# Ten of a tile's nineteen left-over V groups moved from beside the attention to beside the recurrence, and a few dots moved the other way

## The chip, the cores and the metric

The kernel runs on one core of one Trainium2 chip. The metric is the device time of one execution in microseconds (us); lower is better. The five engines of the core work side by side, each through its own list of instructions in order: TensorE (PE, with its weight loads as PEld), VectorE (DVE), ScalarE (ACT), GpSimd (POOL) and SyncE (SP). An engine waits for another one only where its list holds a wait on a semaphore. Sixteen DMA engines move the data between the chip's memory and the on-chip memories.

## What is computed

One inference step of an encoder with one layer: 16 meta tokens, 512 prompt tokens and 64 sample tokens go through a norm and one input projection; eight attention heads and, beside them, four heads of a gated recurrence; an output projection and a residual; then a retrieval layer. Cut to what matters here, the retrieval of one tile of tokens is:

```python
q = (xb @ w_query).reshape(T, 8, 2, 128)
s = einsum('thcd,hcnd->thcn', q, sub_keys)          # scores against 2 x 128 keys
sa, ia = top_k(s[:, :, 0], 16); sb, ib = top_k(s[:, :, 1], 16)
...                                                 # best 16 of the 256 sums per head -> eidx (128 per token), gate
act = gelu(einsum('thkd,td->thk', expert_u[eidx], xb))   # one dot product per token and slot: row of U
return einsum('thk,thkd->td', gate * act, expert_v[eidx]) # weighted sum of rows of V
```

Each token picks 128 of 16384 experts, and each expert is a row of 1024 floats in U and one in V. So every tile of 128 tokens fetches 128 x 128 rows of U and as many of V, at addresses that are known only after the top-k.

## The kernel before

The tokens are cut into five tiles: tile 0 holds the sample and the meta tokens, tiles 1 to 4 hold 128 prompt tokens each. All engines run a loop over the tiles `t = 0..4`. A pass of it has these stages, which I name here as the tables in the code do: `start` and `head0` to `head7` (the attention, eight heads), `subtract`, `levels`, `multiply`, `masks` and `gram0` to `gram3` (the recurrence, done in chunks with one set of Gram matmuls per head), `out` (output projection), `rows` (norm, query projection, scores) and `top` (the top-k, on DVE).

The retrieval of a tile is carried out inside the passes that follow. One gather (POOL, an indirect DMA, line 589 for U and 595 for V) brings one row for each of 128 tokens: 128 x 4096 bytes = 0.524 MB. A U gather is used up by one **dot** on DVE (line 1384, a multiply with a sum over 1024 columns). Four V gathers are used up by one **V group** (the code says quad): ACT makes four 128x32 diagonals out of the weights (line 817, a ring of 8), and PE runs matmuls with them over the rows (line 1041), summing into PD. A tile has 128 U gathers and 32 V groups (tile 0 half of each).

In pass `t` stand: the dots of tile `t-1`, spread over the stages by `DOT_PLACES`; at `top`, the first 13 V groups of tile `t-1` (16 in pass 1, all of tile 0's); and in passes 3 and 4 the other 19 V groups of tile `t-2`, spread by `LEFT_PLACES`. Pass 1 has half the dots, with each number halved and rounded down, and `rows` gets what is left. What is left of tiles 3 and 4 comes after the last pass.

All gathers are issued by POOL in one order, which is worked out from the two tables, and land in a ring of slots; a gather waits until the dot or V group that used its slot before has been done:

```python
quads = len(of_values) // QUAD
for i in range(max(1, quads)):
    for k in of_keys[len(of_keys) * i // max(1, quads):len(of_keys) * (i + 1) // max(1, quads)]:
        u_place[k] = len(order)
        order.append((t, k, None))
    for n in of_values[i * QUAD:(i + 1) * QUAD]:
        v_place[n] = len(order)
        order.append((t, None, n))
...
    slot = i % FIRST_RING if i < SLOTS // 2 else (i - SLOTS // 2 + FIRST_RING) % RING
```

So inside a place the dots are dealt out over its V groups, the ring has `RING = 17` slots (for the 64 dots of pass 1 only `FIRST_RING = 5`), and a tile's first gather also waits for `chosen`, the end of that tile's top-k.

What stands around the moved work, by engine: PE does in a head `scores` (line 1099), `turn_probs` (1110), the head's V groups, `values` (1118). Then come the transposes for the recurrence (1153 to 1157), the V groups of `levels`, a transpose (1165) that waits for `lev_mul`, the V groups of `masks`, and per recurrent head the Gram matmuls (1181, 1182) and, one head later, its outputs (1189, 1191); V groups of `gram1` and `gram2` stand between the outputs of one head and the Gram matmuls of the next. DVE masks and reduces a head's Gram (1519, 1521) and then does the dots of that place; the Gram matmuls of the next head wait for the reduce. ACT does the exponential of the recurrence (903) behind the diagonals of `levels`, and copies the finished sum PD out (914) behind those of `gram2`.

Of the kernel before, what the change touches and what calls it, by code (L numbers as in the profile page):

```python
# [37 lines left out]
HEADS = 8  # L38
# [3 lines left out]
HG = 4  # L42
# [36 lines left out]

DOT_PLACES = [("start", 7)] + [(f"head{h}", 7) for h in range(HEADS)] + [
    ("subtract", 3), ("levels", 5), ("multiply", 3), ("masks", 4)] + [(f"gram{h}", 3) for h in range(HG)] + [
    ("out", 12), ("rows", 26)]
LEFT_PLACES = [("start", 2)] + [(f"head{h}", 2) for h in range(HEADS)] + [
    ("levels", 1)]
NEXT_PLACES = [("top", 13)]

FIRST_NEXT = 16
# [24 lines left out]
def build(nc, x_prompt, x_sample, cache_kt, cache_v, cache_logf, state_hgrn, meta_tokens, w_in,  # L114
# [4 lines left out]
    with ExitStack() as ctx:  # L119
# [205 lines left out]
        def columns_of(t):  # L325

            first = (S_GROUPS + T_GROUPS * (t - 1)) * GROUP
            return range(first, first + SLOTS) if t else range(SLOTS // 2)
# [17 lines left out]
        def values_before(t):  # L346

            return SLOTS // 2 + SLOTS * (t - 1) if t else 0
# [6 lines left out]
        for t in range(1, TILES):  # L355
            cols, taken = columns_of(t - 1), 0
            for place, n in DOT_PLACES:
                n = n * len(cols) // SLOTS if place != DOT_PLACES[-1][0] else len(cols) - taken
                dots_at[t, place] = cols[taken:taken + n]
# [4 lines left out]
            if t > 2:  # L364
                first, left, quads_before = values_before(t - 2) + n_next, SLOTS - n_next, 0
                of_tile = (values_before(t - 1) - first) // QUAD
                for place, quads in LEFT_PLACES:
                    taken = of_tile * quads_before * QUAD // left
# [16 lines left out]
        for t in range(1, TILES + 1):  # L385
            for place in [place for place, _ in DOT_PLACES + NEXT_PLACES] + ["end", "last", "rest"]:
                of_keys, of_values = dots_at.get((t, place), ()), values_at.get((t, place), ())
# [1330 lines left out]
```

## Time and profile before

| | us |
|---|---|
| time, median of 3 runs | 2190.84 (2189.47 to 2190.89) |
| the profiled execution: its own time | 2188.74 |
| its span, first to last instruction | 2186.6 |
| DVE busy | 1261.9 |
| PE busy | 1222.7 |
| POOL busy | 1166.5 |
| ACT busy | 372.6 |
| data moved by DMA | 722.04 MB, 330 GB/s over the span |

No engine is busy for more than 58% of the span. The granted TensorE clock was 0.738 of full speed on the mean. Of the 722 MB, 624.01 went through the queue that the gathers use. What is between the span and the execution's time (2.1 us) is not part of the trace.

### The profile page before, as it was taken

How to read it: one execution, taken by the hardware profiler on the slowest of the kernel's cores; microseconds unless marked ns; L12 is line 12 of the kernel's file. 1: busy time of each engine (PE TensorE's matmuls, PEld its weight loads, DVE VectorE, ACT ScalarE, POOL GpSimd, SP SyncE). 2: the span in 40 equal slices, each digit the busy share in tenths (PEclk: the TensorE clock that was granted, in tenths of full speed). 3: DMA queues.
4: the chain of work that ended last, by engine and by line, in shares of the span. 5: the costliest groups of instructions: out<-in, count | busy, mean ns of one | idle time of the engine just before them, and what ended most of it. 6: DMA issues, size and time to landing. Idle time of an engine off the chain costs nothing.

```text
span 2186.6 us, 15704 instructions
## 1 busy us (share of the span) xinstructions
PE 1222.7 (56%) x4932; PEld 548.7 (25%) x4932; DVE 1261.9 (58%) x2795; ACT 372.6 (17%) x1034; POOL 1166.5 (53%) x1197
## 2 busy tenths in 40 slices
PE   5898777555864436744553675466467322223553
PEld 2544343234321333311123331123323000000110
DVE  3344331866595997765439786544977656565001
ACT  1221211121121111311111131111113100001211
POOL 3012110232477754577774457777445767777773
PEclk9798889776998567866656786666578656555787
DMA  9211183556899989999998999999899999999997
GB/s 331 99 59 59 58 297 119 186 201 221 331 410 409 409 331 397 378 377 409 409 409 328 397 390 376 409 409 409 305 397 352 374 409 409 409 410 409 411 409 294
DMA packets 204306, 722.04 MB, mean 330 GB/s; under 512 B 23248, under 2 KB 25536, under 8 KB 203072
## 3 DMA queue, kind: packets, MB, share of 16 engines
q0 software_dynamic: 171168, 624.01, 73.5%
q1 hardware_dynamic: 33056, 97.03, 12.2%
q8 instruction: 40, 0.66, 0.1%
q14 instruction: 42, 0.34, 0.0%
HBM read 704.71 MB, written 15.70 MB: 329 GB/s over the span
## 4 chain that ended last, share of the span: by engine, by line
DMA 26%; PE 24%; DVE 16%; POOL 13%; issue 5%; ACT 4%; DVEq 0%; POOLq 0%; ACTq 0%
DMA arena<-peer_expert_v,idx_v 16%; POOL arena L595 8%; DMA arena<-peer_expert_u,idx_all 7%; DVE arena L1384 7%; PE PD L1041 5%; POOL arena L589 4%; PE PB L1251 4%; PE PD L963 3%; PE PB L1230 2%; PE PA L1181 2%; PE PA L1230 2%; DMA lev<-w_out 2%; DMA lev<-peer_w_query 2%; DVE w L1521 2%; PE PA L1041 1%
## 5 line engine op out<-in xcount | busy, mean ns | idle before, releaser
L589 POOL DMA_INDIRECT arena<-peer_expert_u,idx_all x576 | 542.5, 942 | 507.7 <-DVE arena L1384 259.6
L1384 DVE SCALAR_TENSOR_TENSOR arena<-arena,PC 128x1024 f32<-128x1024 f32 x576 | 677.1, 1217 | 142.8 <-DMA arena<-peer_expert_u,idx_all 135.6
L595 POOL DMA_INDIRECT arena<-peer_expert_v,idx_v x576 | 567.3, 985 | 228.7 <-issue 143.1
L1041 PE MATMUL PD<-arena,diag_v 128*32 128x512 f32 x1792 | 365.6, 897 | 497.6 <-DMA arena<-peer_expert_v,idx_v 436.5
L1041 PEld LDWEIGHTS PD<-arena,diag_v 128*32 128x32 f32 x1792 | 80.0, 141 | 749.8 <-issue 749.8
L817 ACT ACTIVATE diag_v<-consts,gate_all 128x32 f32<-128x32 f32 x576 | 136.7, 309 | 535.0 <-PE PD L1041 410.7
L963 PE MATMUL PD<-arena 128*128 128x512 f32 x384 | 174.6, 610 | 0.0
L1449 DVE TENSOR_TENSOR PA<-PA,consts 128x128 f32<-128x128 f32 (+4 forms) x56 | 14.0, 250 | 219.9 <-PE PA L1099 219.6
L1041 PE MATMUL PA<-arena,diag_v 128*32 128x512 f32 x512 | 85.5, 800 | 80.3 <-DMA arena<-peer_expert_v,idx_v 80.3
L963 PEld LDWEIGHTS PD<-arena 128*128 128x128 f32 x384 | 73.4, 196 | 85.9 <-issue 85.3
L1230 PE MATMUL PB<-lev,rows_t 128*128 128x512 f32 x160 | 83.0, 672 | 11.0 <-ACT rows_t L922 5.6
L1251 PE MATMUL PB<-arena,rows_t 128*128 128x512 f32 (+1 forms) x160 | 81.8, 676 | 5.6 <-ACT rows_t L926 5.6
L1118 PE MATMUL PB<-v_pr,w 128*128 128x64 f32 (+1 forms) x224 | 52.1, 378 | 48.4 <-ACT w L876 48.4
L857 ACT ACTIVATE w<-PA,small 64x576 f32<-64x576 f32 (+5 forms) x48 | 25.2, 526 | 294.0 <-DVE small L1452 287.6
L1230 PE MATMUL PA<-lev,rows_t 128*128 128x512 f32 (+1 forms) x160 | 72.5, 600 | 4.9 <-DMA lev<-peer_w_query 4.9
L1644 DVE TENSOR_TENSOR lev<-lev,PD 128x1024 f32<-128x1024 f32 x1 | 1.2, 1222 | 126.3 <-PE PA L1041 126.3
L1181 PE MATMUL PA<-lev 128*128 128x128 f32 x248 | 52.3, 394 | 34.4 <-DVE w L1521 34.4
L1118 PEld LDWEIGHTS PB<-v_pr,w 128*128 128x128 f32 (+1 forms) x224 | 43.6, 268 | 82.6 <-ACT w L876 53.1
L1181 PEld LDWEIGHTS PA<-lev 128*128 128x128 f32 x248 | 48.6, 297 | 38.2 <-DVE w L1521 23.1
L1165 PE MATMUL PB<-consts,lev 128*128 128x128 f32 x20 | 5.4, 426 | 94.0 <-DVE lev L1512 94.0
L1041 PEld LDWEIGHTS PA<-arena,diag_v 128*32 128x32 f32 x512 | 18.8, 131 | 147.8 <-issue 147.8
L648 POOL DMA_DIRECT2D arena<-w_in x4 | 3.6, 899 | 93.0 <-PE PD L963 93.0
(271 smaller groups left out, 1527.4 us busy)
## 6 DMA issues: line engine op xcount, KB each, us to landing
lev<-w_out SPq DMA_DIRECT2D x40, 512.0 KB, 8.1
lev<-peer_w_query SPq DMA_DIRECT2D x40, 512.0 KB, 8.1
arena<-w_in SPq DMA_DIRECT2D x8, 2048.0 KB, 14.3
arena<-peer_expert_u,idx_all POOLq DMA_INDIRECT x576, 11.2
arena<-peer_expert_v,idx_v POOLq DMA_INDIRECT x576, 11.4
arena<-w_in POOLq DMA_DIRECT2D x4, 2048.0 KB, 8.8
act<-staged SPq DMA_DIRECT2D x4, 1796.0 KB
staged<-arena POOLq DMA_DIRECT2D x5, 1024.0 KB, 5.5
```

The source lines that it names most:

```text
L589: pool.indirect_dma_start(slot, None, peer_expert_u[0], bass.IndirectOffsetOnAxis(ap=idx_all[:, k:k + 1], axis=0)).then_inc(arrived, 16)
L595: pool.indirect_dma_start(slot, None, peer_expert_v[0], bass.IndirectOffsetOnAxis(ap=idx_v[:, k:k + 1], axis=0)).then_inc(arrived, 16)
L817: return eng.activation(diag_v[:, at * STRIP:(at + 1) * STRIP], consts[:, C_FOLD:C_FOLD + STRIP], ACT.Copy, scale=gate_all[:, k:k + 1])
L857: eng.activation(w1[0:m, D * (a % 2):D * (a % 2) + n], score_psum(a, n)[0:m, :], ACT.Exp, bias=negmax[0:m, h:h + 1], accum_out=psums[0:m, ...
L963: last = pe.matmul(out, x[:, c * P:(c + 1) * P], weights[:, c, :], start=(c == 0), stop=(c == DC - 1))
L1041: ins = pe.matmul(psum[c * STRIP:(c + 1) * STRIP, half * 512:(half + 1) * 512], diag_v[:, at * STRIP:(at + 1) * STRIP], ring[slot_of[v_pla ...
L1118: last = pe.matmul(attended(t)[0:m, h * HD:(h + 1) * HD], w2[0:k, at:at + m], value_rows(t, q0, i, k, h // (HEADS // KV_HEADS)), start=(i ...
L1181: pe.matmul(psum[:, l * P:(l + 1) * P], both, both, start=True, stop=True)
L1230: last = pe.matmul(out[:, half * 512:(half + 1) * 512], rows_t[:, c % DC * P:c % DC * P + n], w_out_sb[:, slot, half * 512:(half + 1) * 51 ...
L1251: last = pe.matmul(PB[0:nq, half * 512:half * 512 + 512], rows_t[:, c * P:c * P + nq], w_query_sb[:, c, half * 512:half * 512 + 512], star ...
L1384: eng.scalar_tensor_tensor(out=slot, in0=slot, scalar=1.0, in1=h2_dots[:, :], op0=ALU.mult, op1=ALU.mult, accum_out=out).then_inc(free, 1)
L1521: eng.tensor_reduce(w1[:, D + HW + h * P:D + HW + (h + 1) * P], masked[:, c0:D].rearrange("p (l q) -> p q l", q=P), AX_X, ALU.add).then_in ...
```

## The change

Two tables of numbers change, nothing else:

```diff
-DOT_PLACES = [("start", 7)] + [(f"head{h}", 7) for h in range(HEADS)] + [
-    ("subtract", 3), ("levels", 5), ("multiply", 3), ("masks", 4)] + [(f"gram{h}", 3) for h in range(HG)] + [
-    ("out", 12), ("rows", 26)]
-LEFT_PLACES = [("start", 2)] + [(f"head{h}", 2) for h in range(HEADS)] + [
-    ("levels", 1)]
+DOT_PLACES = [("start", 8)] + [(f"head{h}", 8) for h in range(HEADS)] + [
+    ("subtract", 2), ("levels", 4), ("multiply", 2), ("masks", 3)] + [(f"gram{h}", 2) for h in range(HG)] + [
+    ("out", 12), ("rows", 25)]
+LEFT_PLACES = [("start", 1)] + [(f"head{h}", 1) for h in range(HEADS)] + [
+    ("levels", 3), ("masks", 3), ("gram1", 2), ("gram2", 2)]
```

Counted out per pass (dots + V groups, and the gathers that these are):

| pass | attention | recurrence | out | rows |
|---|---|---|---|---|
| 1 before | 27 dots | 10 dots | 6 | 21 |
| 1 after | 36 dots | 9 dots | 6 | 13 |
| 2 before | 63 dots | 27 dots | 12 | 26 |
| 2 after | 72 dots | 19 dots | 12 | 25 |
| 3 and 4 before | 63 dots + 18 groups = 135 gathers | 27 dots + 1 group = 31 gathers | 12 | 26 |
| 3 and 4 after | 72 dots + 9 groups = 108 gathers | 19 dots + 10 groups = 59 gathers | 12 | 25 |

POOL in pass 3, from `head7` on (U gathers by line 589, V gathers by 595; the last row of before also holds the later stages). Before:

```order
L589 DMA arena<-peer_expert_u,idx_all 128x1024 x3
L595 DMA arena<-peer_expert_v,idx_v 128x1024 x4
L589 DMA arena<-peer_expert_u,idx_all 128x1024 x4
L595 DMA arena<-peer_expert_v,idx_v 128x1024 x4
L589 DMA arena<-peer_expert_u,idx_all 128x1024 x8
L595 DMA arena<-peer_expert_v,idx_v 128x1024 x4
L589 DMA arena<-peer_expert_u,idx_all 128x1024 x57
```

With the change, from `head7` to the first group of `masks`:

```order
L589 DMA arena<-peer_expert_u,idx_all 128x1024 x8
L595 DMA arena<-peer_expert_v,idx_v 128x1024 x4
L589 DMA arena<-peer_expert_u,idx_all 128x1024 x3
L595 DMA arena<-peer_expert_v,idx_v 128x1024 x4
L589 DMA arena<-peer_expert_u,idx_all 128x1024
L595 DMA arena<-peer_expert_v,idx_v 128x1024 x4
L589 DMA arena<-peer_expert_u,idx_all 128x1024 x2
L595 DMA arena<-peer_expert_v,idx_v 128x1024 x4
L589 DMA arena<-peer_expert_u,idx_all 128x1024 x3
L595 DMA arena<-peer_expert_v,idx_v 128x1024 x4
```

A head's gathers went from 7 U and 8 V to 8 U and 4 V, and V gathers now stand between those of the recurrence's dots.

PE in pass 3 from the V groups of `levels` to the third head's Gram matmuls. Before:

```order
L1041 MATMUL PD<-arena,diag_v 32x512 x8
L1165 MATMUL PB<-consts,lev 128x128 x4
L1181 MATMUL PA<-lev 128x128 x7
L1182 MATMUL PA<-w 128x128
L1181 MATMUL PA<-lev 128x128 x7
L1182 MATMUL PA<-w 128x128
L1189 MATMUL PB<-act,w 128x128
L1191 MATMUL PB<-state,lev 128x128
L1181 MATMUL PA<-lev 128x128 x7
```

With the change:

```order
L1041 MATMUL PD<-arena,diag_v 32x512 x24
L1165 MATMUL PB<-consts,lev 128x128 x4
L1041 MATMUL PD<-arena,diag_v 32x512 x24
L1181 MATMUL PA<-lev 128x128 x7
L1182 MATMUL PA<-w 128x128
L1181 MATMUL PA<-lev 128x128 x7
L1182 MATMUL PA<-w 128x128
L1189 MATMUL PB<-act,w 128x128
L1191 MATMUL PB<-state,lev 128x128
L1041 MATMUL PD<-arena,diag_v 32x512 x16
L1181 MATMUL PA<-lev 128x128 x7
```

Three V groups (8 instructions each here, 16 in the trace) now stand ahead of the first Gram matmuls, and two ahead of those of the third head; two more stand ahead of the fourth's.

DVE in pass 1, around the dots of `rows`, as a piece of the difference:

```order
 L1561 SCALAR_TENSOR_TENSOR rows<-w,small 128x1024
-L1384 SCALAR_TENSOR_TENSOR arena,dots_all<-arena,PC 128x1024 x21
+L1384 SCALAR_TENSOR_TENSOR arena,dots_all<-arena,PC 128x1024 x13
 L1401 TENSOR_TENSOR dots_all<-dots_all,gate_all 128x64
 L1577 MAX lev<-PB 128x8 x8
```

Eight of tile 0's dots left this place for the attention of pass 1.

## Rows read from the trace of the kernel before

**Rows 1.** The page's slices: GB/s in 40 equal slices of the span.

```profile
GB/s 331 99 59 59 58 297 119 186 201 221 331 410 409 409 331 397 378 377 409 409 409 328 397 390 376 409 409 409 305 397 352 374 409 409 409 410 409 411 409 294
```

**Rows 2.** Stretches: length, busy PE, PEld, DVE, ACT, POOL; granted clock, DMA share, GB/s.

```profile
685.30:766.30 81.00, 29.37 (x104) 22.08 (x104) 80.40 (x154) 9.06 (x33) 61.16 (x66) 0.54 1.03 409
969.00:1146.40 177.40, 87.40 (x406) 31.59 (x406) 84.05 (x154) 26.03 (x105) 133.36 (x143) 0.63 1.03 409
1146.40:1159.50 13.10, 6.03 (x29) 2.83 (x28) 9.13 (x23) 2.34 (x6) 4.25 (x5) 0.63 1.02 404
1159.50:1174.75 15.25, 0.00 (x0) 0.00 (x0) 15.21 (x35) 4.04 (x1) 10.78 (x11) 0.50 0.92 330
1174.75:1203.00 28.25, 16.50 (x80) 15.80 (x80) 27.48 (x34) 1.51 (x2) 13.14 (x15) 0.74 0.82 296
1203.00:1213.80 10.80, 2.93 (x12) 2.63 (x12) 8.72 (x21) 3.57 (x5) 2.82 (x3) 0.66 0.95 356
1350.40:1530.20 179.80, 97.55 (x445) 40.00 (x446) 85.27 (x162) 28.51 (x105) 134.11 (x143) 0.69 1.03 409
1530.20:1598.20 68.00, 25.60 (x121) 20.81 (x120) 60.48 (x110) 11.47 (x14) 29.62 (x31) 0.55 0.87 314
```

**Rows 3.** Costliest groups: the wait of the V groups on PE.

```profile
L1041 PE MATMUL PD<-arena,diag_v 128*32 128x512 f32 x1792 | 365.6, 897 | 497.6 <-DMA arena<-peer_expert_v,idx_v 436.5 <-ACT diag_v L817 61.1
```

**Rows 4.** Order of time, PE in pass 3: start, us, what, [idle before].

```profile
1138.25 3.50 PE L1041 MATMUL PD<-arena,diag_v 128*32 128x512 f32 x16 [5.03 <-DMA arena<-peer_expert_v,idx_v]
...
1174.89 1.09 PE L1165 MATMUL PB<-consts,lev 128*128 128x128 f32 x4 [17.64 <-DVE lev L1512]
...
1182.59 3.33 PE L1181 MATMUL PA<-lev 128*128 128x128 f32 x14 [3.31 <-DVE w L1521]
1185.71 0.45 PE L1182 MATMUL PA<-w 128*128 128x128 f32 x2
...
1203.04 0.80 PE L1189 MATMUL PB<-act,w 128*128 128x128 f32 x2 [2.78 <-DVE w L1521]
```

**Rows 5.** Order of time, DVE in pass 3.

```profile
1153.06 1.21 DVE L1384 SCALAR_TENSOR_TENSOR arena<-arena,PC 128x1024 f32<-128x1024 f32 x1
1154.20 1.21 DVE L1384 SCALAR_TENSOR_TENSOR arena<-arena,PC 128x1024 f32<-128x1024 f32 x1
...
1159.43 1.21 DVE L1384 SCALAR_TENSOR_TENSOR arena<-arena,PC 128x1024 f32<-128x1024 f32 x1
...
1179.31 1.22 DVE L1519 TENSOR_TENSOR w<-PA,level_masks 128x1024 f32<-128x1024 f32 x1
```

**Rows 6.** Order of time, POOL in pass 3.

```profile
1154.55 0.94 POOL L589 DMA_INDIRECT arena<-peer_expert_u,idx_all  x1 [6.48 <-DVE arena L1384]
...
1165.89 1.15 POOL L589 DMA_INDIRECT arena<-peer_expert_u,idx_all  x1 [0.30 <-issue]
...
1289.52 0.94 POOL L595 DMA_INDIRECT arena<-peer_expert_v,idx_v  x1 [14.98 <-PE PD L1041]
...
1320.50 2.50 POOL L595 DMA_INDIRECT arena<-peer_expert_v,idx_v  x1 [0.31 <-issue]
```

**Rows 7.** DMA issues: KB each, median us from issue to landing.

```profile
arena<-peer_expert_u,idx_all POOLq DMA_INDIRECT x576, 11.2
...
w<-x_prompt SPq DMA_DIRECT2D x4, 512.0 KB, 4.1
```

**Rows 8.** The chain that ended last: one V group.

```profile
1303.61 1.98 PE PD L1041 x16
```

**Rows 9.** Order of time in pass 1: DVE at `head6`, POOL and PE at `top`.

```profile
461.77 0.30 DVE L1449 TENSOR_TENSOR PA<-PA,consts 128x128 f32<-128x128 f32 x1 [3.86 <-PE PA L1099]
...
606.68 0.94 POOL L595 DMA_INDIRECT arena<-peer_expert_v,idx_v  x1 [0.48 <-PE PD L1041]
...
670.26 0.94 POOL L595 DMA_INDIRECT arena<-peer_expert_v,idx_v  x1 [0.30 <-issue]
...
680.22 3.63 PE L1041 MATMUL PD<-arena,diag_v 128*32 128x512 f32 x16 [1.49 <-DMA arena<-peer_expert_v,idx_v]
```

## The prediction, made before the changed kernel was run

> **What bounds the kernel now.** I began with the page's slices: from a quarter of the span on, the DMA engines move 409 to 411 GB/s in most slices and never more, so that is their ceiling here; single slices fall to 305 to 397 [rows 1]. A gather is 0.524 MB, so at 409 GB/s one takes 1.28 us. The costliest groups say who feels it: V groups on PE waited 437 us for their rows, the longest wait of a group [rows 3]. Then I cut passes 2, 3 and 4 into stages [rows 2]. The attention of passes 3 and 4 runs at 409 GB/s from end to end (177.4 and 179.8 us), though DVE and PE are busy for half of it: it is as long as its 135 gathers. The recurrence behind it is another case: 404, 330, 296 and 356 GB/s in pass 3 and 314 on the mean in pass 4, and DVE is busy for nearly all of it (15.21 of 15.25 us, 27.48 of 28.25). It has 31 gathers and room for more. So the change takes gathers from where DMA sets the end to where it doesn't. The last views are lists in order of time, for the recurrence of pass 3.
>
> **Passes 3 and 4: attention.** It loses 27 gathers of 1.28 us: 34.6 us. Does it stay bound by DMA? A head has 8 dots, of which one starts every 1.14 us [rows 5], thus 9.1 us, beside 12 gathers, 15.4 us: yes. On before's clock the attention of pass 3 now ends at 1146.4 - 34.6 = 1111.8, and its last V rows, which PE waited for until 1138.25 [rows 4], land at 1103.6.
>
> **Passes 3 and 4: recurrence.** It has 57 gathers up to the last V row of `gram2`, 73 us at the ceiling. What can starve the DMA is the ring: a gather needs the slot of the one 17 places ahead. POOL stood for 6.48 us until the first dot of `subtract` gave its slot back [rows 6], and yet the stretch moved 404 GB/s [rows 2]: what was in flight covered it. The tightest place now is the first dot of `levels` (place 111 of the pass): it runs at 1159.43 [rows 5] less 34.6, less one dot of `subtract` (1.14), and frees its slot at 1124.9. Gather 128, which waits for it, would land at 1103.6 + 20 x 1.28 = 1129.2 if nothing starved. How long a gather takes from issue to landing when few others are in flight, no row shows: between 4.1 us (a load of as many bytes that is issued into a quiet queue) and the 11.2 us median of gathers [rows 7]. That makes a loss of 0 to 6.9 us; I take 1.5, near the quiet end, since the queue is nearly empty by then. So gather 128 lands at 1130.7 and the last V row of `masks`, 15 later, at 1149.9.
>
> From there PE's order counts, since the groups stand ahead of the Gram matmuls. A group takes 3.5 to 3.6 us [rows 4, 9] at the low clock; a head's Gram matmuls 3.57 (1182.59 to 1186.16) and its outputs 0.8 [rows 4]; DVE's mask and reduce 3.28 (1179.31 [rows 5] to PE's start at 1182.59 [rows 4]). In order: third group of `masks` 1153.5; Gram of head 0 1157.1; reduce 1160.3; Gram of head 1 1163.9; outputs 1164.7; two groups of `gram1`, whose rows have landed (1149.9 + 12 x 1.28 = 1165.3 for the second) 1171.9; Gram of head 2 1175.5 (its reduce was done at 1167.2); outputs 1176.3; groups of `gram2` 1179.9 and 1183.5 (last row landed at 1178.1); Gram of head 3 1187.1; reduce 1190.4. Before, that reduce let PE go on at 1203.04 [rows 4]: -12.6 us. One dot fewer in `gram3` gives between nothing and 1.14, as PE's last matmuls run beside it: -0.5. Against it, the five loads of w_out that are issued here meet gathers that before had landed: +1.0 (bounds in the rival of the debt, below), and gathers beside DVE's products are issued more slowly: +0.5 (below). Pass 3: **-11.6**. Pass 4 has the same gathers, and from its attention to the end of its recurrence it took 68.0 us where pass 3 took 67.4 [rows 2]: **-11.6**.
>
> ACT's 12 diagonals of `levels` stand ahead of its exponential and wait for PE's first group there, whose rows land at 1103.6 + 7 x 1.28 = 1112.6; the exponential's input comes at about 1123.7, and that time hides them. Were the group later than that, DVE's products would be late by as much. SP's list is the same, and no queue is passed. The 26th dot of `rows` isn't on a path: PE's projections end that stage.
>
> **Pass 2 pays.** It has no left-over groups, so it only gets 9 dots more beside the attention, which DVE fills (80.40 of 81.00 us [rows 2]): 9 x 1.14 = +10.3. Its recurrence loses 8 dots: one each in `subtract`, `levels` and `multiply`, which are DVE's chain (-3.4); one in `masks` and one per Gram, beside which PE's Gram matmuls run (3.57 against 3 dots of 1.14: 0), but 0.5 for the last. Sum **+6.4**; bounds +1.2 (all eight on the path) and +10.3.
>
> **Pass 1 is nearly even.** DVE waits 3.86 us per head for PE's item projections [rows 9], which covers the fourth dot, but not in `start`, `head6` and `head7`: +3.4, and +0.6 because only five slots serve them (0 to 2). In `rows` eight dots fewer are of no use to PE, but POOL comes to the V gathers some 10 us earlier (8 x 1.28). The 18th of them, however, waited for PE's first group even before (0.48 us at 606.68 [rows 9]); so the 64th is issued at 670.26 as now, and only its landing gets shorter: 10.0 us now (PE had waited for it until 680.22), 4.1 at best [rows 7]. Gain 0 to 5.9; I take 3. Sum **+1**.
>
> Sum: +1 + 6.4 - 11.6 - 11.6 = -15.8, so 2188.74 - 15.8 = 2172.9 against the profiled execution. That execution is 2.1 us below the median of the runs, so I forecast **2175 us**.
>
> The 0.5 for slower issue: beside DVE's large products of the top-k a gather's issue took 2.50 us instead of 0.94, beside the short products of the recurrence 1.15 [rows 6]. Some five issues per pass meet such products; by the row they lose 0.2 us each at most, 1.0, and I took half. The Trainium skill (SBUF — State Buffer, "Who interferes with whom") has a rule that speaks against gathers in this place: a DVE instruction with two SBUF inputs and a GpSimd instruction that reads SBUF exclude each other. By it I estimate that each of the five waits out a whole product of 0.4 us: 2 us per pass, and 2178 in all.
>
> **The rivals.**
> *A faster PE* (0.2). A V group took 1.98 us where PE had worked just before [rows 8]. The granted clock was 0.74 beside the Gram matmuls and 0.50 (1.2 GHz) in the stretch without matmuls before them [rows 2]; groups in that stretch may lift it. Then the groups no longer hold PE, and the last rows do: 1178.1 + 2.0 + 3.6 + 3.3 = 1187.0 for the last reduce, 3.4 us more per pass, 2168. The Trainium skill (TensorE: Matmul & The Clock Gate, Part 1) has the clock released by activity, which would go this way.
> *The ring starves the DMA* (0.1, the slow side). If the stretch keeps the rate that it had, 330 GB/s for 56.6 us of pass 3 [rows 2], its 57 gathers (29.9 MB) take 90.6 us instead of 74.6: +16 in each pass, 2207. It decides from 7.9 us per pass on, that is below 362 GB/s. For it speaks POOL's stop of 6.48 us; against it, that DVE was busy all through: the rate was low since few rows were asked for.
> *The debt comes due* (0.08). Before, all 17 slots hold landed rows when the recurrence ends; then about 9, and 8 x 1.28 = 10.3 us of DMA work is left to stages that run at 400 and more. If `out` and the projections wait for all of it, both passes keep 2.3 us: 2194, no change. Against it: POOL stood idle for 14.98 us until 1289.52 with a full ring, before the next V groups began [rows 6]; that is where the debt can be paid.
> Other (0.05): the change does nothing because another wait takes over in the attention, e.g. DVE behind PE's group.
>
> **Numbers.** Forecast as summed 0.57, 2166 to 2185. This measurement tells about 0.2%, 4.4 us, from no change. Faster 0.8 (forecast, faster PE, a little of the rest), same 0.1, slower 0.1. Range 2163 to 2188: from the faster PE with all of the gain in pass 1 and a little more in pass 2, to 6.5 us lost per pass in the ring; the slow rivals lie above.
>
> **What would show it.** Right: attention of passes 3 and 4 about 143 and 145 us at 409 GB/s; from its end to the last reduce about 78 us instead of 57, at 385 GB/s or more; the attention of pass 2 91 us; PE's groups in `masks` waiting for DMA and those in `gram1` not. Wrong: POOL standing for over 8 us in the recurrence, released by the dots of `levels` or of a Gram; `out` longer by over 4 us; or DVE dots, not V rows, ending a head.

## The result and the profile after

The changed kernel takes **2177.36 us** (median of 5 runs, 2174.77 to 2179.58), the kernel before 2190.89 in the same job: ratio 0.9925, 95% interval 0.9909 to 0.9941. It is faster by 13.5 us on the medians and by 10.7 us between the profiled executions (2178.01 and 2188.74; spans 2175.9 and 2186.6). The 3 us between these two are chance: the attention of pass 0, which the tables don't touch, took 107.96 us in the profile of before, 111.86 in that of after, and 110.65 in the control with the tables of before (below).

Cut at PE's last transposes of the queries (line 1060), the profiles give per pass:

| | before | after | difference | predicted |
|---|---|---|---|---|
| ahead of pass 1 | 389.72 | 392.99 | +3.3 | 0 |
| pass 1 | 295.56 | 296.74 | +1.2 | +1 |
| pass 2 | 283.74 | 292.09 | +8.4 | +6.4 |
| pass 3 | 381.37 | 369.18 | -12.2 | -11.6 |
| pass 4 and what follows, to DVE's last instruction | 833.08 | 821.76 | -11.3 | -11.6 |

The tables don't touch what stands ahead of pass 1, so its 3.3 us are no effect of the change; passes 1 to 4 together gained 13.9 us.

The windows that answer to [rows 2], with the same columns: attention of pass 2; attention, `subtract` with `levels` up to the products, `multiply`, Grams, mix and `out` of pass 3; attention, its end to the last reduce, and `out` of pass 4.

```profile
689.71:781.03 91.32, 29.61 (x105) 22.13 (x104) 90.69 (x172) 9.96 (x34) 69.08 (x74) 0.53 1.03 409
981.80:1122.37 140.57, 59.20 (x262) 25.33 (x262) 92.45 (x172) 18.41 (x69) 106.44 (x113) 0.62 1.03 409
1122.37:1134.42 12.05, 7.81 (x45) 3.72 (x44) 8.01 (x22) 4.15 (x14) 4.23 (x5) 0.77 1.02 398
1134.42:1147.41 12.99, 2.74 (x16) 0.50 (x16) 12.96 (x31) 4.05 (x1) 9.13 (x9) 0.64 0.86 311
1147.41:1200.39 52.98, 32.98 (x192) 15.37 (x192) 23.22 (x27) 8.09 (x30) 39.88 (x44) 0.77 1.02 408
1200.39:1210.12 9.73, 1.60 (x12) 1.42 (x12) 7.63 (x20) 3.57 (x5) 5.86 (x6) 0.81 1.03 410
1210.12:1238.65 28.53, 19.55 (x40) 8.69 (x40) 14.93 (x26) 2.31 (x2) 11.32 (x12) 0.77 1.03 410
1350.98:1495.24 144.26, 64.46 (x305) 31.57 (x305) 94.84 (x180) 20.91 (x69) 109.11 (x116) 0.66 1.03 409
1495.24:1572.26 77.02, 44.91 (x250) 20.11 (x248) 44.17 (x76) 16.29 (x45) 53.84 (x57) 0.73 1.01 398
1582.73:1609.86 27.13, 20.98 (x40) 9.01 (x40) 14.92 (x26) 2.31 (x2) 11.32 (x12) 0.77 1.03 410
```

The attention of pass 3 lost 36.8 us (177.4 to 140.6) and still stands at the ceiling. The stretch of the Grams, which ran at 296 GB/s, runs at 408 and takes 52.98 us instead of 28.25. The mix (the last step of the recurrence, ahead of `out`) went from 356 to 410 GB/s. And `out`, where nothing was moved, is new on the list: 28.53 us. Its window of before, not shown so far, has 21.99:

```profile
1213.80:1235.79 21.99, 18.25 (x40) 7.96 (x40) 14.91 (x26) 2.31 (x2) 11.27 (x12) 0.86 1.00 403
```

Out of these two windows: 410 x 28.53 us = 11.70 MB were moved in it after, 403 x 21.99 = 8.86 MB before. The 2.84 MB more take 6.9 us at 410 GB/s.

What waits there, on PE, in order of time as in [rows 4]. First before, then after; line 1230 is the output projection, in blocks of w_out of which each is four matmuls:

```profile
1216.96 10.33 PE L1230 MATMUL PB<-lev,rows_t 128*128 128x512 f32 x20 [1.11 <-ACT rows_t L922]
1227.46 1.98 PE L1230 MATMUL PB<-lev,rows_t 128*128 128x512 f32 x4 [0.17 <-DMA lev<-w_out]
1230.00 1.98 PE L1230 MATMUL PB<-lev,rows_t 128*128 128x512 f32 x4 [0.56 <-DMA lev<-w_out]
```

```profile
1213.27 10.48 PE L1230 MATMUL PB<-lev,rows_t 128*128 128x512 f32 x20 [1.11 <-ACT rows_t L922]
1230.30 7.10 PE L1230 MATMUL PB<-lev,rows_t 128*128 128x512 f32 x12 [6.55 <-DMA lev<-w_out]
```

The first five blocks are there in time. The sixth is late by 6.55 us; the two behind it come just as PE gets to them. SP's own list, in order of time, says what stands ahead of that block (after):

```profile
1200.43 0.33 SPq L517 DMA_DIRECT2D w<-x_prompt  x1
1201.20 2.23 SPq L525 DMA_DIRECT2D lev<-w_out  x5
1210.16 0.33 SPq L534 DMA_DIRECT2D w<-norm_gain  x1
1210.53 0.43 SPq L537 DMA_DIRECT2D act<-sub_keys_t  x1
1216.91 3.76 SPq L525 DMA_DIRECT2D lev<-w_out  x3
```

How long some of these took to land (after; KB each, us from issue): the fifth block (issued at 1203.0), the gain, the keys, the sixth block:

```profile
lev<-w_out SPq DMA_DIRECT2D x1, 512.0 KB, 18.4
w<-norm_gain SPq DMA_DIRECT2D x1, 512.0 KB, 13.7
act<-sub_keys_t SPq DMA_DIRECT2D x1, 1024.0 KB, 17.2
lev<-w_out SPq DMA_DIRECT2D x1, 512.0 KB, 13.3
```

So they landed one behind the other, at 1221.4, 1223.9, 1227.7 and 1230.2: between the fifth and the sixth block 6.3 us went to the gain and the keys. PE was through with the fifth block at 1223.75; without these 6.3 us the sixth would, by this sum, have been there at 1223.9. The list was late before that, too: counted from its first load (`x_prompt`, issued at 1203.01 before and at 1200.43 after), the fifth block landed after 16.0 us before and after 20.9 with the change, the sixth after 24.4 and 29.8.

The DMA queues' packets and MB (third column: packets' time as a share of 16 engines) in the first 9 to 12 us of `out`, before and then after; q1 is SP's queue, q0 that of the gathers:

```profile
q1 hardware_dynamic: 557, 2.51, 68.4%
q0 software_dynamic: 262, 0.97, 26.6%
```

```profile
q1 hardware_dynamic: 668, 2.45, 51.6%
q0 software_dynamic: 665, 2.43, 51.4%
```

Before, in 9.0 us (1213.8 to 1222.8), SP's queue got 279 GB/s, since the gathers' queue had work for only a part of the time (POOL had stood for 7.28 us until 1215.23). After, in 11.9 us (1210.1 to 1222), both got the same: 206 and 204 GB/s. The same shows ahead of `out`, where the first five blocks come: from 1205 to 1208 us, SP's queue moved 224 packets and that of the gathers 18 before, 165 and 167 after.

In the recurrence PE waits as follows (after, from the products on, in order of time):

```profile
1147.57 1.09 PE L1165 MATMUL PB<-consts,lev 128*128 128x128 f32 x4 [7.73 <-DVE lev L1512]
1150.28 3.64 PE L1041 MATMUL PD<-arena,diag_v 128*32 128x512 f32 x16 [1.62 <-ACT diag_v L817]
1155.16 3.58 PE L1041 MATMUL PD<-arena,diag_v 128*32 128x512 f32 x16 [1.25 <-DMA arena<-peer_expert_v,idx_v]
1161.96 3.60 PE L1041 MATMUL PD<-arena,diag_v 128*32 128x512 f32 x16 [3.21 <-DMA arena<-peer_expert_v,idx_v]
1165.49 1.83 PE L1181 MATMUL PA<-lev 128*128 128x128 f32 x14
...
1174.15 2.63 PE L1041 MATMUL PD<-arena,diag_v 128*32 128x512 f32 x16
1177.99 1.92 PE L1041 MATMUL PD<-arena,diag_v 128*32 128x512 f32 x16 [1.21 <-ACT diag_v L817]
...
1184.39 1.92 PE L1041 MATMUL PD<-arena,diag_v 128*32 128x512 f32 x16 [2.05 <-DMA arena<-peer_expert_v,idx_v]
1190.80 3.64 PE L1041 MATMUL PD<-arena,diag_v 128*32 128x512 f32 x16 [4.48 <-DMA arena<-peer_expert_v,idx_v]
...
1200.46 0.49 PE L1189 MATMUL PB<-act,w 128*128 128x128 f32 x2 [2.77 <-DVE w L1521]
```

The second and third group of `masks` and both of `gram2` wait for their rows, those of `gram1` don't (the first of `masks` and the second of `gram1` wait for ACT's diagonals). The two places at which POOL stood there, in order of time as in [rows 6]:

```profile
1130.61 0.94 POOL L595 DMA_INDIRECT arena<-peer_expert_v,idx_v  x1 [5.45 <-DVE arena L1384]
...
1135.84 0.94 POOL L589 DMA_INDIRECT arena<-peer_expert_u,idx_all  x1 [2.88 <-DVE arena L1384]
```

And how long the ten gathers that were issued from 1130.6 to 1144.7 took to land, from the answer on their tile:

```profile
L595 POOL DMA_INDIRECT arena<-peer_expert_v,idx_v x6: 940/950/1163, 1130.6 to 1144.7; - x6
...
DMA to landing us min/median/max: 5.8/6.1/6.3
```

### The profile page after: what moved, and what is told of

It reads as the page before. It is cut to its first block, busy times and chain, and to the rows that moved or that the text cites. A ratio compares the mean times of both kernels' runs of the same rounds, so it can differ in the third digit from the quotient of the medians.

```text
span 2175.9 us, 15704 instructions
## 1 busy us (share of the span) xinstructions
PE 1216.6 (56%) x4932; PEld 541.1 (25%) x4932; DVE 1261.5 (58%) x2795; ACT 374.3 (17%) x1034; POOL 1174.1 (54%) x1197
## 4 chain that ended last, share of the span: by engine, by line
PE 25%; DMA 24%; DVE 16%; POOL 14%; issue 5%; ACT 4%; DVEq 0%; POOLq 0%; ACTq 0%
DMA arena<-peer_expert_v,idx_v 16%; POOL arena L595 10%; DVE arena L1384 7%; PE PD L1041 6%; DMA arena<-peer_expert_u,idx_all 5%; POOL arena L589 4%; PE PB L1251 4%; PE PD L963 3%; PE PB L1230 3%; PE PA L1230 2%; DMA lev<-w_out 2%; PE PA L1181 2%; DMA lev<-peer_w_query 2%; DVE w L1521 1%; DVE lev L1501 1%
## 5 line engine op out<-in xcount | busy, mean ns | idle before, releaser
L1230 PE MATMUL PB<-lev,rows_t 128*128 128x512 f32 x160 | 86.6, 700 | 18.1 <-DMA lev<-w_out 12.4
L1644 DVE TENSOR_TENSOR lev<-lev,PD 128x1024 f32<-128x1024 f32 x1 | 1.2, 1222 | 127.6 <-PE PA L1041 127.6
L1519 DVE TENSOR_TENSOR w<-PA,level_masks 128x1024 f32<-128x1024 f32 (+1 forms) x18 | 21.8, 1210 | 78.8 <-PE PA L1182 78.8
L1181 PE MATMUL PA<-lev 128*128 128x128 f32 x248 | 47.2, 364 | 23.5 <-DVE w L1521 23.5
L1181 PEld LDWEIGHTS PA<-lev 128*128 128x128 f32 x248 | 43.6, 270 | 34.5 <-issue 23.3
## 6 DMA issues: line engine op xcount, KB each, us to landing
arena<-peer_expert_v,idx_v POOLq DMA_INDIRECT x576, 10.2
```

The lines of the kernel that those rows point to most:

```text
L1181: pe.matmul(psum[:, l * P:(l + 1) * P], both, both, start=True, stop=True)
L1230: last = pe.matmul(out[:, half * 512:(half + 1) * 512], rows_t[:, c % DC * P:c % DC * P + n], w_out_sb[:, slot, half * 512:(half + 1) * 51 ...
L1519: link(eng.tensor_tensor(masked[:, c0:D], gram_psum(t, h)[:, c0:D], level_masks[:, c0:D], ALU.mult))
```

## The experiments

Ten kernels. Beside each its median and its ratio to the kernel before of the same job; in pass 3 the attention, its end to the end of the mix, and `out`, in us:

| | time | ratio (95%) | attention | to mix | `out` |
|---|---|---|---|---|---|
| before, four jobs | 2190.89, 2194.24, 2191.58, 2192.8 | | 177.4 | 67.4 | 22.0 |
| the change | 2177.36 | 0.9925 (0.9909 to 0.9941) | 140.6 | 87.8 | 28.5 |
| 1 groups only | 2168.35 | 0.989 (0.9873 to 0.9907) | 130.1 | 97.4 | 28.6 |
| 2 dots only | 2212.82 | 1.0091 (1.0075 to 1.0106) | 191.2 | 63.4 | 22.3 |
| 3 new dots in passes 3, 4 only | 2169.65 | 0.9897 (0.988 to 0.9915) | 141.4 | 87.1 | 28.5 |
| 4 gathers held back | 2177.2 | 0.9924 (0.9909 to 0.9939) | 143.2 | 86.2 | 29.3 |
| 5 change, keys late | 2166.98 | 0.9881 (0.9864 to 0.9898) | 142.6 | 88.7 | 21.7 |
| 6 groups only, keys late | 2155.95 | 0.984 (0.9821 to 0.986) | 129.9 | 97.2 | 22.3 |
| 7 six groups | 2174.42 | 0.9919 (0.9905 to 0.9933) | 150.7 | 86.1 | 22.4 |
| 8 before, keys late | 2191.53 | 0.9996 (0.9985 to 1.0008) | 178.1 | 68.0 | 22.3 |
| 9 as 6, rows 30 | 2148.36 | 0.9796 (0.9783 to 0.9809) | 127.1 | 97.0 | 22.4 |
| 10 as 6, twelve groups | 2153.58 | 0.9819 (0.9805 to 0.9832) | 118.7 | 107.4 | 22.3 |

**1 and 2: the two halves of the change.** Each takes one of the two tables from the change and the other from before: kernel 1 has the new `LEFT_PLACES` and the old `DOT_PLACES`, kernel 2 the reverse.

> The ten V groups move, the dots stay where they were. Theory (gathers leave the attention, which DMA bounds, for the recurrence, where DMA has room; the dots' move only costs passes 1 and 2): passes 1 and 2 go back to before (-7 us against the changed kernel), the attention of passes 3 and 4 has 99 gathers, thus about 129 and 133 us, and the recurrence 67, thus DMA-bound for about 9 us longer than with the change. 2166 to 2173 us, faster than the change. Rival (the dots had to leave the recurrence to make room for the groups): the recurrence of passes 3 and 4 grows by 15 us or more each and eats what passes 1 and 2 give back: 2178 or more.

> The dots move, the V groups stay. Theory: pass 1 costs 2, pass 2 5.5, and in passes 3 and 4 the attention has 144 gathers instead of 135 (+11.5 each) against 5 us less in the recurrence: 2190.9 + 2 + 5.5 + 13 = 2211 us. Rival (what is saved comes from dots that leave DVE's chain in the recurrence): no slower than before, 2191 or less.

Measured 2168.35 and 2212.82. By the ratios the groups alone bring 1.1%, some 24 us, and the dots alone cost 0.9%, some 20. Added to the groups the dots cost 9.0 us on the medians, which come from two jobs, and 0.35% or 8 us by the ratios. Both theories hold.

**3: the dots of before in passes 1 and 2, those of the change in passes 3 and 4** (`EARLY_DOT_PLACES` is the table of before).

```diff
-            for place, n in DOT_PLACES:
+            for place, n in (EARLY_DOT_PLACES if t < 3 else DOT_PLACES):
```

> Both new tables in passes 3 and 4, the old table of dots in passes 1 and 2. Theory: the gain of passes 3 and 4 stays, the price of passes 1 and 2 goes: 2177.4 - 7.4 = 2170 us (2167 to 2173). Rival (what pass 2 pays comes back later, since its rows are fetched earlier): 2177.

Measured 2169.65, the groups alone 2168.35 (their ranges overlap): in passes 3 and 4 the moved dots are worth nothing that these runs can tell once the groups are moved, and their cost lies in the two passes that have no left-over groups.

**4: POOL waits before the sixth dot gather of `rows`** until PE has used three blocks of w_out.

```diff
                 slot_free(i)
+                if k is not None and t >= 3 and k in dots_at.get((t, "rows"), ()) and k == dots_at[t, "rows"][5]:
+                    pool.wait_ge(wo_used, 2 * DC * t + 3)
```

> The changed kernel with one wait more on POOL in passes 3 and 4: the gathers from the sixth dot of rows on wait until PE has used three blocks of w_out. Theory (out got longer by 6.5 and 4.6 us because the loads of w_out queue behind gathers that the recurrence left in flight): PE's 6.6 us wait for w_out falls to about 1, out is back at 22 to 23 us, and nothing is lost behind, where POOL has 15 us of idle time: 2166 to 2170 us. Rival (the loads are late for another reason, or the held gathers make rows or top late by as much): 2176 to 2179.

Measured 2177.2: no change, the rival was right. POOL did stand, yet PE still waited for the sixth block:

```profile
1221.24 0.94 POOL L589 DMA_INDIRECT arena<-peer_expert_u,idx_all  x1 [12.07 <-DVE arena L1386]
```

```profile
1229.68 8.19 PE L1232 MATMUL PB<-lev,rows_t 128*128 128x512 f32 x12 [5.28 <-DMA lev<-w_out]
```

Its queues from 1209.8 to 1221.8 show why: the gathers issued earlier keep their queue filled, and it takes its half all the same (203 GB/s). The last gather ahead of the stop, issued at 1207.75, took 20.6 us and landed at 1228.3, 1.4 us before PE had the sixth block:

```profile
arena<-peer_expert_u,idx_all POOLq DMA_INDIRECT x1, 20.6
```

```profile
q1 hardware_dynamic: 663, 2.47, 51.5%
q0 software_dynamic: 667, 2.43, 51.0%
```

**5, 6 and 8: SP issues the norm gain (0.5 MB) and the keys (1 MB) behind blocks 6 to 8 of w_out**, in the change, in the groups alone, and in the kernel before as a control.

```diff
+                for c in range(WO_RING, DC):
+                    sp.wait_ge(wo_used, 2 * DC * t + c - WO_RING + 1)
+                    load_w_out(c)
                 sp.dma_start(gain_2, ...
...
                 sp.dma_start(keys_t, sub_keys_t).then_inc(keys_in, 16)
-                for c in range(WO_RING, DC + WO_RING):
+                for c in range(DC, DC + WO_RING):
```

> The changed kernel, but SyncE issues the norm gain (0.5 MB) and the keys (1 MB) behind the w_out blocks 6 to 8 and not ahead of them; they are needed only later (norm, scores). Theory: the sixth w_out block is late in passes 3 and 4 because of the bytes that stand ahead of it, the 1.5 MB of SyncE's own list among them (3.8 us at 409 GB/s): the stage out falls from 28.5 and 27.1 us to about 24.5 and 24 us, PE's wait for that block from 6.6 us to about 3, and the time from 2177.4 to 2170 to 2173 us. Rival: gathers alone fill the path and SyncE's own order is worth nothing: 2176 to 2179, PE's wait stays above 5 us.

> Only the V groups moved (dots as before the change), with the same late keys and gain. Theory: the gain adds up with that of the groups alone (2168.35 us): 2162 to 2165. Rival: 2167 to 2170, as the groups alone.

> The kernel before with the late keys and gain only. Theory: its rows have landed when w_out is loaded and PE waits for no block by more than 0.6 us, so it gains nothing that can be told: 2188 to 2192. Rival: the order of SyncE's list costs in every pass, whatever the groups do: 2186 or less.

Measured 2166.98, 2155.95 and 2191.53: -10.4 on the change and -12.4 on the groups alone (10 and 11 us by the ratios), nothing on before. PE's waits in `out` of pass 3 in kernel 5:

```profile
1212.35 12.17 PE L1233 MATMUL PB<-lev,rows_t 128*128 128x512 f32 x24 [1.11 <-ACT rows_t L925]
1225.09 1.98 PE L1233 MATMUL PB<-lev,rows_t 128*128 128x512 f32 x4 [0.58 <-DMA lev<-w_out]
```

The sixth block is in the unbroken run of 24, and `out` is 21.67 us in pass 3 and 22.88 in pass 4 (28.53 and 27.12 with the change): -6.9 and -4.2, about the whole difference in time. The theory had the cause right and the size too small, in kernel 6 too: it priced the 1.5 MB at the full 409 GB/s (3.8 us), but SP's queue has to share, and with the change the gain and the keys took 6.3 us of it. The Trainium skill (DMA: Bandwidth & Descriptors, "Queues, rings and completion order") says that each DMA engine goes round between the queues that have work, a packet at a time. The trace agrees: 668 and 665 packets above, and equal numbers of packets even where the bytes differ. While the keys landed (after, 1223.9 to 1227.7) the two queues moved

```profile
q1 hardware_dynamic: 177, 0.88, 56.7%
q0 software_dynamic: 182, 0.66, 43.6%
```

that is, 5.0 KB to a packet on SP's side and 3.6 on the gathers'.

**7: six groups moved instead of ten** (dots of before; compare kernel 1).

```diff
-LEFT_PLACES = [("start", 1)] + [(f"head{h}", 1) for h in range(HEADS)] + [
-    ("levels", 3), ("masks", 3), ("gram1", 2), ("gram2", 2)]
+LEFT_PLACES = [("start", 1)] + [(f"head{h}", 1) for h in range(4)] + [(f"head{h}", 2) for h in range(4, HEADS)] + [
+    ("levels", 3), ("masks", 3)]
```

> Dots as before the change, six V groups moved to the recurrence and not ten: three each in levels and masks, none between the Grams; heads 4 to 7 keep two. Theory: the groups that stand between the Grams are the ones that gain, since the 16 gathers that return to the attention (20.5 us) come out of a stretch that then has few left, and the four rounds of Gram and reduce (some 27 us) run with few gathers landing; out gets back about 4 us of its 6: some 6 us per pass slower than ten groups alone (2168.35), 2177 to 2184. Rival: the debt in out is what the last four groups cost, and six gain as much or more: 2170 or less.

Measured 2174.42, between the two forecasts: +6.1, so 3 per pass. In pass 3 the attention is longer by 20.6 and the part up to the mix shorter by 11.3, as expected (+9.3); but `out` gives back 6.1 and not 4. Against kernel 6, whose `out` is as short, the four groups between the Grams are worth 18.5 us, or 9.2 per pass. So the theory was right on what these groups gain, and the rival on half of it: `out` pays for them.

**9: four dots out of the attention into `rows`** (kernel 6 otherwise).

```diff
-DOT_PLACES = [("start", 7)] + [(f"head{h}", 7) for h in range(HEADS)] + [
+DOT_PLACES = [("start", 7)] + [(f"head{h}", 7 - h % 2) for h in range(HEADS)] + [
...
-    ("out", 12), ("rows", 26)]
+    ("out", 12), ("rows", 30)]
```

> Ten groups moved, keys and gain late (2155.95 us), and four dots more moved the opposite way to the change: one each out of head1, head3, head5 and head7 into rows (26 to 30; pass 1 unchanged, as halves are rounded down). Theory: dots cost 1.28 us each in the attention of passes 3 and 4, where DMA sets the end, and 1.14 in that of pass 2, where DVE does, and nothing in rows, where DVE is busy for 30.35 of 40.35 us and POOL stands for 13.42 us behind it: -14.8 us, 2139 to 2145. Rival: their 2 MB in rows take the rows of the first V groups of top with them, and top pays: 2150 to 2156.

Measured 2148.36, -7.6, half of what the theory gave and more than the rival: the fastest kernel here. Its profiled execution is the longest of its six (2157.95, 2.0 above kernel 6's): it took 8.4 us more up to pass 2, where the edit changes nothing, and 6.2 less from there on. So the stages are compared from pass 2 on. The attentions of passes 2, 3 and 4 lost 4.6, 2.8 and 6.6 us, 14.0 together and nearly what was forecast. But in pass 3 the stretch from the top-k's end to the start of pass 4 went from 10.50 to 17.17 us, which takes 6.7 back:

```profile
1323.84:1341.01 17.17, 10.11 (x60) 3.09 (x60) 0.83 (x4) 3.46 (x7) 12.91 (x14) 0.80 1.03 410
```

It now runs at the ceiling (410 GB/s, 392 in kernel 6), and so does the top-k ahead of it (410 and 406): POOL's stop behind `rows` fell from 13.42 to 8.19 us, with one of 3.31 behind it, and most of what the dots put back there comes out at the other end. The attentions went as the theory had it, and the rival's cost came in pass 3.

**10: twelve groups** (kernel 6 otherwise).

```diff
-LEFT_PLACES = [("start", 1)] + [(f"head{h}", 1) for h in range(HEADS)] + [
-    ("levels", 3), ("masks", 3), ("gram1", 2), ("gram2", 2)]
+LEFT_PLACES = [("start", 1)] + [(f"head{h}", 1) for h in range(6)] + [
+    ("levels", 3), ("masks", 3), ("gram1", 3), ("gram2", 3)]
```

> Keys and gain late and the dots of before, but twelve groups moved: head6 and head7 have none, gram1 and gram2 three each. Theory: from the start of the attention to the last V row of gram2 the path is at its ceiling (409 GB/s), so that row is the same one in the count of gathers and the last Gram comes no sooner: same as ten groups with late keys, 2153 to 2159. Rival: each group more brings what the ten brought on the mean, (2191.6 - 2156.0) / 10 = 3.6 us: 2149 or less.

Measured 2153.58 (2152.22 to 2153.89) against 2155.95 (2152.89 to 2161.18): the same within the spread, as the theory said. In pass 3 the attention gave 11.1 us and the part up to the mix took 10.2 back. With the path at 409 GB/s up to the last V row of `gram2`, it made no difference on which side of the attention's end these two groups stand.

## Why the prediction was right, and where not

The time (2177.4 against 2175, range 2163 to 2188) and the sum of each pass came out. The terms inside a pass did not all do so.

**Attention of passes 3 and 4.** 27 gathers of 1.28 us gave -34.6; measured -36.8 and -35.5, at 409 GB/s, with PE waiting for V rows ahead of each of the nine groups (7.33 to 10.95 us in pass 3). Right. "DVE dots, not V rows, ending a head", a sign against it, did not come.

**Recurrence of passes 3 and 4.** From the attention's end to the last reduce 78.0 and 77.0 us; forecast 78. The rate over it is 390 GB/s in pass 3 (4.80 + 4.04 + 21.6 MB in 78.0 us), above the 362 from which the starving ring would decide. The unknown landing time of a gather in a quiet queue is 6.1 us, within 4.1 to 11.2 and near the quiet end, as taken. POOL stood for 5.45 and 2.88 us, released by the first dot of `subtract` (ends at 1130.33) and the first of `levels` (1135.56); of the 8 us named as a sign against the forecast, "released by the dots of `levels` or of a Gram", only the 2.88 came.

**PE's order** was right in its result and not in its holder. Shifted by the attention's real end (1122.37 instead of 1111.8), the chain put the end of the second `gram2` group at 1194.1 and the last reduce at 1201.0; measured 1194.4 and 1200.4. But the chain had PE at 3.6 us a group and the rows landed; the rows held it (2.05 and 4.48 us of waiting), since PE was faster. The windows of the third group of `masks`, of the first Gram behind it and of the second group of `gram2` say at which level:

```profile
1161.96:1165.49 3.53, 3.53 (x17) 0.67 (x17) 0.00 (x0) 0.00 (x0) 2.62 (x4) 0.52 1.03 410
1165.49:1167.50 2.01, 2.01 (x20) 1.86 (x16) 0.00 (x0) 0.96 (x4) 1.61 (x2) 1.00 1.02 408
...
1190.80:1194.40 3.60, 3.60 (x17) 0.68 (x17) 0.00 (x0) 0.00 (x0) 2.69 (x4) 0.50 1.02 409
```

The groups of `masks` still ran at 1.2 GHz (0.52). Behind the last of them the clock was at 2.4 (1.00): the Gram took 1.83 us instead of 3.33 [rows 4], and three of the four groups after it 1.92 to 2.63. After PE's wait of 4.48 us it was low again (0.50). The rival of the faster PE had the engine right and the time wrong, as the rows came some 2 us later than it assumed, and the clock had fallen again by then.

**`out`: the step that was mis-sized.** "The five loads of w_out that are issued here meet gathers that before had landed: +1.0" measured +6.5 in pass 3 and +4.6 in pass 4. It counted five blocks, and these were in time for PE, though 5 us later in their queue; behind them on SP stand the gain and the keys and then three blocks more, and these wait for all that is ahead of them. "SP's list is the same", the prediction says, and leaves it at that: the list is the same, but its order began to cost. With the gathers' queue no longer empty for long, SP's queue gets about half the path. The rival of the debt had named this stage and its 10.3 us of left-over transfers, and hence "`out` longer by over 4 us" as a sign against the forecast: it came. Kernels 5, 6 and 8 show the cause: with SP's order changed, `out` is as short as before, and the debt is paid later, where it costs little (from the end of `out` to the top-k's end pass 3 took 102.6 us in kernel 5 and 102.4 before). Kernel 4 shows that it isn't the gathers that POOL issues at that time, but those that are in flight already.

**Why the sum held all the same.** Up to the end of the mix passes 3 and 4 gained 16.5 and 16.0 us; the sum had 12.6. The attention gave 2.2 and 0.9 more, the rest up to the mix 1.7 and 2.5. With `out` this leaves -9.9 and -11.4; the stretches behind it gave 2.3 more in pass 3 (the time from the top-k's end to the next pass was 9.58 us instead of 12.19; at the end of passes 2 and 3 it lies between 9.6 and 13.5 in these two kernels and in 1 to 8 and 10). So two misses of opposite signs met, and that the total came within 2.4 us is in part luck.

**Pass 2** paid +10.3 in the attention, as forecast to a tenth. Its recurrence gave back 4.8 (forecast 3.9), and the step from the top-k's end into pass 3 took 2.2 more (11.30 to 13.53), which no step had and which lies within the same spread. **Pass 1**: attention +4.4 (forecast 4.0, the right size by a wrong count: DVE's wait of 3.86 us [rows 9] stands ahead of `head3` to `head6` alone, so four heads hide a fourth dot and not six); from the top-k's end to pass 2 27.13 to 24.83, -2.3 (forecast -3, bounds 0 and 5.9).

**Slower issue.** Nine gathers in `multiply` took 9.13 us on POOL, 1.01 each against 0.94: 0.7 us in all, and 0.5 was taken. The rule on the shared port in the Trainium skill (SBUF — State Buffer, "Who interferes with whom") had given 2 us and 2178 in all. The time is near that, but not for its reason: waits for whole products would have shown as 1.3 us and more on five gathers, and one took 1.30, the next 1.16. Beside the top-k's products of 2.29 us, which also read two tensors in SBUF, the trace of before does agree with the rule: gathers issued at 1320.50 and 1328.12 took 2.50 and 2.16 us and were through 0.8 us after the product that they had met. Beside the products of 0.42 us the most that was added is 0.36 (1.30).

**By its parts** the change is the groups, some 24 us below before by the ratio, and the dots, 8 to 9 us on top of them, nearly all of it in pass 2 (+8.4) and pass 1 (+1.2).

## What to carry to other kernels

When transfers move into a stretch that had room on the path, price not only that stretch but the next load that another queue must land: write down that queue's whole list in order, with bytes, and count it at about half the path for as long as the other queue has work. A load that is needed late but stands early in such a list costs nothing while the path is free and some microseconds a pass once it isn't: its reordering brought some 10 us on the change and nothing without it. And where the path was full from end to end, moving two more groups within it gave nothing (kernel 10); only what lies behind the last transfer that is waited for counts.

## What was not expected of the hardware

Two DMA queues that both had work shared the path packet by packet, and so by halves where their packets were alike: 2.45 and 2.43 MB in 11.9 us with the change, 2.47 and 2.43 in 12.0 us with gathers held back. With larger packets on one side the bytes differ (0.88 and 0.66 MB in 177 and 182 packets). A gather of 0.524 MB with few others in flight (about five, at one issued every 1.25 us) lands 5.8 to 6.3 us after its issue, where the median of all was 11.2 [rows 7].
